# Up-projection of a two-part float32 feed-forward: high weights against the tokens' high and low parts in one product of 512 columns

## The reference, cut to what matters

```python
def squared_relu_mlp(x, w_up, w_down):
    return jnp.square(jax.nn.relu(x @ w_up)) @ w_down

def second_block(x, ...):
    h = x
    ...
    h = h + rms_norm_2(u, norm_mix_post[layer])
    u = squared_relu_mlp(rms_norm_2(h, norm_ffn_pre[layer]), w_up[layer], w_down[layer])
    h = h + rms_norm_2(u, norm_ffn_post[layer])
```

## Time and profile before

| | us |
|---|---|
| three runs | 970.64, 977.29, 977.51 |
| median | 977.29 |
| profiled execution: span from first to last instruction | 971.9 |
| profiled execution: its own time | not listed apart from the span |
| TensorE products busy | 934.8 (96%) |
| TensorE weight loads busy | 633.1 (65%) |
| VectorE busy | 443.5 (46%) |
| ScalarE busy | 351.2 (36%) |

### The profile page before, as it was taken

One profiled execution on the slowest core, in us unless ns is written; L12 is line 12 of the kernel. 1 busy time (PEld: TensorE's weight loads), 2 busy tenths in 40 slices (PEclk: granted clock), 3 DMA queues, 4 the chain that ended last, 5 costly groups with the idle time before them and its releaser, 6 DMA issues.

```text
span 971.9 us, 12898 instructions
## 1 busy us (share of the span) xinstructions
PE 934.8 (96%) x5259; PEld 633.1 (65%) x5259; DVE 443.5 (46%) x761; ACT 351.2 (36%) x568; POOL 25.9 (3%) x40
## 2 busy tenths in 40 slices
PE   7999999998999999999999999888999989999997
PEld 6979889885444443444434443333999889998886
DVE  5887665435232322223222322214776656655444
ACT  6745565532221121221212211115554454454332
POOL 1310000000000000000000000000000000000000
PEclk9999999999999999999999999999999999999999
DMA  9955553479999999999999999999944645555501
GB/s 317 359 191 170 172 173 130 173 272 409 401 429 426 426 428 430 424 430 427 428 428 425 428 427 430 426 428 374 355 154 153 196 129 175 174 182 205 176 1 44
DMA packets 72638, 289.81 MB, mean 298 GB/s; under 512 B 5121, under 2 KB 44673, under 8 KB 59650
## 3 DMA queue, kind: packets, MB, share of 16 engines
q1 hardware_dynamic: 72002, 288.79, 76.3%
q10 hardware_dynamic: 576, 0.17, 0.1%
HBM read 287.90 MB, written 1.05 MB: 297 GB/s over the span
## 4 chain that ended last, share of the span: by engine, by line
PE 83%; DMA 9%; DVE 3%; ACT 3%; issue 2%; POOL 0%; DVEq 0%; ACTq 0%
PE bank L1599 19%; PE bank L455 14%; PE bank L456 14%; PE bank L457 14%; PE bank L1621 10%; DMA ring<-in_w_gate_up_second 5%; DMA ring<-in_attn_w_qkv 4%; PE bank L1571 3%; PE bank L1637 3%; ACT w_high L520 1%; DVE w_low L552 1%; PE bank L755 1%; PE bank L793 1%; PE bank L510 1%; PE bank L1610 1%
## 5 line engine op out<-in xcount | busy, mean ns | idle before, releaser
L552 DVE TENSOR_TENSOR w_low<-ring,w_high 128x2048 fp32r<-128x2048 f32 x76 | 174.0, 2289 | 109.6 <-ACT w_high L520 109.5
L1599 PE MATMUL bank<-ring,arena 128*64 128x512 f32 x928 | 207.2, 595 | 7.3 <-DMA ring<-in_w_gate_up_second 6.0
L520 ACT ACTIVATE w_high<-ring 128x2048 fp32r<-128x2048 f32 x76 | 145.4, 1915 | 138.4 <-PE bank L457 136.2
L1599 PEld LDWEIGHTS bank<-ring,arena 128*64 128x64 f32 x928 | 64.8, 137 | 134.9 <-issue 116.9
L455 PE MATMUL bank<-xT_high,w_high 128*128 128x256 f32 x384 | 110.2, 287 | 1.1 <-DVE xT_low L563 1.1
L1736 DVE SCALAR_TENSOR_TENSOR y_low<-bank,arena,y_high 64x512 fp32r<-64x512 f32 x64 | 48.0, 750 | 138.0 <-ACT y_high L1671 137.5
L1621 PE MATMUL bank<-ring,arena 128*64 128x512 f32 x464 | 106.0, 598 | 4.4 <-issue 4.4
L456 PE MATMUL bank<-xT_low,w_high 128*128 128x256 f32 x384 | 109.2, 285 | 0.0
L457 PE MATMUL bank<-xT_high,w_low 128*128 128x256 f32 x384 | 109.2, 284 | 0.0
L1671 ACT ACTIVATE y_high<-bank,arena 64x512 fp32r<-64x512 f32 x64 | 43.7, 683 | 125.8 <-PE bank L1621 125.3
L1658 ACT ACTIVATE arena<-bank 128x256 f32<-128x256 f32 x32 | 12.3, 385 | 192.0 <-PE bank L1599 192.0
(11 more groups left out here) (296 smaller groups left out, 1496.2 us busy)
## 6 DMA issues: line engine op xcount, KB each, us to landing
ring<-in_w_down SPq DMA_DIRECT2D x28, 2048.0 KB, 28.8
ring<-in_w_gate_up_first SPq DMA_DIRECT2D x27, 2048.0 KB, 25.4
ring<-in_w_gate_up_second SPq DMA_DIRECT2D x27, 2048.0 KB, 26.8
ring<-in_w_down SPq DMA_DIRECT2D x18, 1024.0 KB, 5.0
ring<-in_w_up SPq DMA_DIRECT2D x16, 1024.0 KB, 5.3
ring<-in_attn_w_qkv SPq DMA_DIRECT2D x12, 1024.0 KB, 12.9
ring<-in_w_in SPq DMA_DIRECT2D x10, 1024.0 KB, 11.5
ring<-in_w_kv_mem SPq DMA_DIRECT2D x8, 1024.0 KB, 5.7
```

Of the source, the lines that this page charges most:

```text
L520: SC.activation(parts[buffer[0][u]][0][:, :], lanes[n % len(lanes)], ACT.Copy).then_inc(*high.inc(u))
L552: DVE.tensor_tensor(p[1][:, :], lanes[n % len(lanes)], p[0][:, :].bitcast(F32), ALU.subtract).then_inc(*split.inc(u))
L1599: last = PE.matmul(GU[t * SLOTS:(t + 1) * SLOTS, 0:NGU], xs[:, k, :], wgu[:, :, c, t * (DE // JT):(t + 1) * (DE // JT)], start=k == 0, sto ...
```

## The change

For each (n, k) of the up-projection the two products with the high weights (times `xT_high` and times `xT_low`) become one: the moving operand is an access pattern of two runs of 256 (`x_low_high[k]`), low part first, and the output takes a whole bank of 512 columns, low times high in columns 0 to 255, high times high in 256 to 511. The product with the low weights adds into columns 0 to 255 (the small half). So a unit has 16 products of 512 columns and 16 of 256, and two banks, f(i).0 and f(i).1, both opened before its first product. The moving operand's two runs need one tensor over both parts, so `xT_low` and `o_low` change places.

The two halves of a bank are summed as they leave: ScalarE copies the small halves to scratch (`small_sum`, new), VectorE adds the large halves onto them and gives back the banks, then makes the scaled maximum from scratch. Banks of the second block share their semaphores with those of the first (`Count(..., after)`), which frees semaphores for the new counts.

```diff
+f6.0@5 f6.1@6 f7.0@7 f7.1@0 f8.0@1 f8.1@2 f9.0@3 f9.1@4 f10.0@5 f10.1@6 f11.0@7 f11.1@0 f12.0@1 f12.1@2 f13.0@3 f13.1@0
+f14.0@4 f14.1@5 f15.0@6 f15.1@7
...
-    bank2 = Banks(nc, SECOND_BANKS, "second_")
-    xT2 = [chunks(rounded("xT_high", 2048, arena_at + 2 * TILE)), chunks(rounded("xT_low", 2048, slot_at(2)))]
+    bank2 = Banks(nc, SECOND_BANKS, bank1)
+    x_span2 = rounded("xT_low_high", (arena_at + 2 * TILE - slot_at(2) - TILE) // 4 + 2048, slot_at(2) + TILE)
+    xT2 = [chunks(x_span2[:, x_span2.shape[1] - 2048:]), chunks(x_span2[:, 0:2048])]
+    x_low_high = [bass.AP(tensor=x_span2, offset=xT2[1][:, k, :].offset,
+                          ap=[xT2[1].ap[0], [x_span2.shape[1] - 2048, 2], [1, S]]) for k in range(KC)]
...
+        def wide_features(u, ready=(), chunk_ready=()):
+
+            PE.wait_ge(*split2.at(u))
+            w_high, w_low = [t[:, :].rearrange("p (c n) -> p c n", c=KC) for t in parts2[buffer2[0][u]]]
+            into = [open_bank(bank2, f"{u}.{n}") for n in range(2)]
+            order = [(n, k) for n in range(2) for k in range(KC)]
+            if ready:
+                order.sort(key=lambda nk: nk[1] // HALF)
+            for n, k in order:
...
+                o = slice(n * P, (n + 1) * P)
+                PE.matmul(into[n][:, :].rearrange("p (l t) -> p l t", t=S), w_high[:, k, o], x_low_high[k], start=k == 0,
+                          stop=False, skip_group_check=True)
+                last = PE.matmul(into[n][:, 0:S], w_low[:, k, o], xT2[0][:, k, :], start=False, stop=k == KC - 1,
+                                 skip_group_check=True)
+            last.then_inc(*unit2.inc(u))
...
+        def small_sum(i):
+            SC.wait_ge(*unit2.at(f"f{i}"))
+            for n in range(2):
+                last = SC.activation(scratch(2 * (i % 2))[:, n * S:(n + 1) * S], banks[bank2.bank[f"f{i}.{n}"]][:, 0:S],
+                                     ACT.Copy)
+            last.then_inc(*small_sums.inc(i))
...
-            SC.wait_ge(*bank2.freed(f"f{i}"))
+            SC.wait_ge(*kept_rows.at(i))
...
+            small_sum(i)
             squared_high(i)
...
         def norm_kept(i):
 
-            if i >= 2:
-                DVE.wait_ge(*sq_high.at(i - 2))
             DVE.wait_ge(*unit2.at(f"f{i}"))
-            DVE.scalar_tensor_tensor(
-                out=scratch(2 * (i % 2)).rearrange("p (n t) -> p n t", t=S),
-                in0=banks[bank2.bank[f"f{i}"]][:, :].rearrange("p (n t) -> p n t", t=S), scalar=0.0,
-                in1=row["r2"].rearrange("p (n t) -> p n t", n=1).to_broadcast([P, 2, S]), op0=ALU.max,
-                op1=ALU.mult).then_inc(*bank2.inc(f"f{i}"))
+            kept = scratch(2 * (i % 2)).rearrange("p (n t) -> p n t", t=S)
+            DVE.wait_ge(*small_sums.at(i))
+            for n in range(2):
+                DVE.tensor_tensor(kept[:, n, :], banks[bank2.bank[f"f{i}.{n}"]][:, S:2 * S], kept[:, n, :],
+                                  ALU.add).then_inc(*bank2.inc(f"f{i}.{n}"))
+            for n in range(2):
+                DVE.wait_ge(*bank2.freed(f"f{i}.{n}"))
+            DVE.scalar_tensor_tensor(out=kept, in0=kept, scalar=0.0,
+                                     in1=row["r2"].rearrange("p (n t) -> p n t", n=1).to_broadcast([P, 2, S]), op0=ALU.max,
+                                     op1=ALU.mult).then_inc(*kept_rows.inc(i))
```

More of the change, by code:

```diff
@@ L27, with __init__ @@
 class Count:
[L30 to L35, removed]
+    def __init__(self, nc, name, order, after=None):
+        self.sem = after.sem if after else nc.alloc_semaphore(name)
+        self.made = after.total if after else 0
+        self.value = {key: self.made + n for n, key in enumerate(order, 1)}
+        self.total = self.made + len(self.value)
     def at(self, key):
@@ L61, with __init__ @@
 class Banks:
-    def __init__(self, nc, plan, prefix):
+    def __init__(self, nc, plan, after=None):
         turn, kept, self.bank = list(range(8)), {}, {}
@@ L82, in __init__ @@
                 kept[name] = b
-        self.free = [Count(nc, f"{prefix}bank{b}_free", uses[b]) for b in range(8)]
+        self.free = [Count(nc, f"bank{b}_free", uses[b], after.free[b] if after else None) for b in range(8)]
     def freed(self, name):
@@ L148 @@
 SECOND_BANKS = """
-+z0@0 +z1@1 +z2@2 +z3@3 -z0 -z1 -z2 -z3
-pT00@4 pT01@5 pT10@6 pT11@7 +v0.0 +v0.1 -v0.0 -v0.1 q0 r1 k0 q1 s0 s1 k1 q2 t0 t1 s2 s3 k2 a0 a1
+pT00@4 pT01@5 pT10@6 pT11@7 +v0.0@0 +v0.1@1 -v0.0 -v0.1 q0 r1 k0 q1 s0 s1 k1 q2 t0 t1 s2 s3 k2 a0 a1
 q3 t2 t3 s4 s5 k3 a2 a3 +v1.0@4 +v1.1@5 t4 t5 s6 s7 +o.0.0@0 +o.0.1@1 +o.1.0@2 +o.1.1@3 -v1.0 -v1.1
 a4@6 a5@7 t6@4 t7@5 a6@6 a7@7 -o.0.0 -o.0.1 -o.1.0 -o.1.1
-fT00@4 fT01@5 fT10@6 fT11@7 f0 f1 r2 f2 f3 f4 f5 f6 f7 f8 f9 f10 f11 f12 f13 f14@0 f15@7
+fT00@4 fT01@5 fT10@6 fT11@7 f0.0@0 f0.1@1 f1.0@2 f1.1@3 r2@4 f2.0@5 f2.1@6 f3.0@7 f3.1@0 f4.0@1 f4.1@2 f5.0@3 f5.1@4
+f6.0@5 f6.1@6 f7.0@7 f7.1@0 f8.0@1 f8.1@2 f9.0@3 f9.1@4 f10.0@5 f10.1@6 f11.0@7 f11.1@0 f12.0@1 f12.1@2 f13.0@3 f13.1@0
+f14.0@4 f14.1@5 f15.0@6 f15.1@7
 +y.0.0@0 +y.0.1@1 +y.1.0@2 +y.1.1@3
@@ L457, in three, with features @@
         return PE.matmul(o, ll, rh, start=False, stop=stop, skip_group_check=True)
-    def features(u, plan, split, unit, parts, buffer, x, ready=(), pairs=slice(0, 2 * KC), chunk_ready=None):
+    def features(u, plan, split, unit, parts, buffer, x, ready=(), pairs=slice(0, 2 * KC)):
         PE.wait_ge(*split.at(u))
@@ L2088, in build_program @@
     sq_low = Count(nc, "squared_low", range(NF))
+    small_sums = Count(nc, "small_sums", range(NF))
+    kept_rows = Count(nc, "kept_features", range(NF))
     added = Count(nc, "added", [f"{t}{h}{j}" for t in ("a", "y") for h in range(NH) for j in range(2)])
@@ L2189, in second_tensor @@
         for h in range(NH):
-            turn_sum("pT", h, XN, [bank2.freed(f"z{2 * h + j}") for j in range(2)], "pT")
+            turn_sum("pT", h, XN, [bank1.freed(f"acc{2 * h + j}") for j in range(2)], "pT")
         open_pair("v0")
@@ L2249, in second_tensor @@
             if i == 0:
-                f("f0", xT2, (("fT00",), ("fT01", "fT11")),
-                  [split2.at(f"eT10.{c}") for c in range(3)] + [bank2.freed("fT10")])
+                wide_features("f0", (("fT00",), ("fT01", "fT11")),
+                              [split2.at(f"eT10.{c}") for c in range(3)] + [bank2.freed("fT10")])
             else:
-                f(f"f{i}", xT2)
+                wide_features(f"f{i}")
             if i == 1:
@@ L2511, in second_vector @@
         DVE.wait_ge(*q.at("scattered", NE // 2))
[L2512 removed]
+        DVE.tensor_scalar(XN[:, 1, 0:512], banks[2][:, :], 1.0, None, ALU.mult).then_inc(*bank1.inc("acc2"))
         DVE.wait_ge(*z_gained.at("columns"))
```

26 lines of the change are left out of this document (14 added, 12 removed).

## The result

The changed kernel takes 983.84 us in the median of four runs (982.65 to 987.17), the kernel before 976.75 (970.64 to 977.51, the three runs told and one more beside). The recorded ratio is **1.0109, 95% interval 1.0087 to 1.013**: slower by about 1%. The two medians are 7.1 us apart, 0.7%, less than the ratio says; the four runs of the kernel before lie 6.9 us apart, so the size is known less well than the sign. The profiled span went from 971.9 to 983.3 us, 11.4 more; the profiled execution after took 984.53. All that follows accounts for the spans.

A forecast was written before the change was run, and what follows sets the result against it. The prediction took TensorE's column streaming to bound the up-projection, and after the change the late low weights. Stalls of 11.69 us less 3.35 saved, 8.3 more, added to the 977.3 median gave 985.6 us, range 975.5 to 990.

The forecast's parts named there:

- The chain: Up-projection: from a unit's end through ScalarE and VectorE to the product needing the low weights, 6.63 us against a 5.55 unit.
- The idle times: TensorE's stalls at f3, f5, f7, f9, f11, f13, f15 and y1, 11.69 us in all.
- The clock: Rival at f13: TensorE's clock falls in the 3.71 us wait, costing 1.6 us, 987.2 in all; chance 0.26.
- f13's hole: TensorE's wait before f13 for the bank that held f11's second half, 3.71 us.
- The saving: TensorE in the up-projection: 16 wide and 16 narrow products a unit instead of 48 narrow, 3.35 us saved.
- the chain doesn't bind: Rival in the up-projection: low weights don't delay TensorE; 977.7, or 973.9 without the bank wait too; chance 0.10.
- the clock falls at every stall: Rival: TensorE's clock drops at each stall, eight times 1.6 us, 998 in all; chance 0.05.
- a wide product costs 0.24: Rival: a 512-column product takes 0.24 us instead of 0.227, so nothing is saved, 987.7; chance 0.08.
- the loads bind: Rival: weight loads limit the up-projection, so fewer of them save 31 us, 946 in all; chance 0.01.
- the last two rivals: Clock falling often (998, chance 0.05) and loads binding (946, chance 0.01), the cases said to lie outside the range.

The follow-up runs named there:

- e2_banks: The changed kernel with another bank plan for f2 to f15, so f13 no longer needs f11's bank: 981.86 us, ratio 1.0096 to the kernel before.
- e5_fill: The changed kernel with 12 idle products on f13's first bank before TensorE waits for the second: 983.60 us, ratio 1.0102 to the kernel before.
- e4_sum_twice: The changed kernel with ScalarE's copies of the small halves made twice, order unchanged: 990.44 us, ratio 1.017 to the kernel before.
- e3_both: The changed kernel with ScalarE's copies ahead of the weights' high part and banks planned by fours: 970.02 us, ratio 0.9964 to the kernel before.
- e7_narrow: The kernel of `e3_both` with each wide product taken apart into two of 256 columns: 973.45 us, ratio 0.9992 to the kernel before.
- e8_low_first: The changed kernel with VectorE making the low part of f(i+3) ahead of the sum of f(i): 994.65 us, ratio 1.02 to the kernel before.
- e1_sum_first: The changed kernel with only ScalarE's copies moved ahead of the high part of f(i+3)'s weights: 970.65 us, ratio 0.9975 to the kernel before.

## Why the prediction was right, and where it was off

The forecast was 985.6 us in a range of 975.5 to 990; it is 983.84. The sign of the change and its cause were as written. That the time came so close is in part luck. The forecast added 8.3 us to a median of 977.29 from three runs 7 us apart, and the spans then grew by 11.4. In the other runs an execution takes 1.2 to 1.3 us longer than its span, so the profiled one before took an estimated 973.1; that and 11.4 give the 984.5 measured. A base 4 us too high and a change 3 us too small nearly cancelled. Step by step:

- **The chain.** Reckoned 6.63 us from the end of a unit to the product that waits for the low part. Measured for f11: ScalarE starts at 848.35 and f11's first product at 854.72, 6.37 later; the start of ScalarE is some 0.25 behind the end of the unit (866.02 + 0.12 to 866.39): 6.62. Its parts were off both ways: VectorE starts 0.1 behind the copies and 0.1 behind its own adds, where I had 0.03 each, and TensorE 0.05 behind VectorE, where I had 0.15.
- **The idle times.** Reckoned 11.69 us at f3, f5, f7, f9, f11, f13, f15 and y1; measured 11.5, at these eight and at no other place. f13's was 3.71 in both.
- **The clock.** I gave the case in which the clock holds through f13's hole 0.40 and the one in which it falls 0.26, and forecast the first. The second came: 1.65 us, reckoned 1.6. `e2_banks` and `e5_fill` show it from both sides, the hole gone and the hole filled, each with the clock at 1.00. This is the step that failed. The evidence is four traces with such a hole or its remedy, one execution each: holes of 3.7 us in the changed kernel and 4.1 in `e4_sum_twice` with half clock behind them, and the clock at 1.00 in the two kernels in which the hole is gone or filled.
- **The saving.** Reckoned 3.35 us. In the changed kernel 1.7 of it is there: idle time of 11.5 and the clock's 1.65 make 13.15, and the two stages are 11.4 longer (10.1 in the up-projection, where "about 7" was forecast, and 1.3 in the down-projection). What is missing lies between the stops. Two units take 11.21, 11.21, 11.41, 11.32 and 11.42 us from start to end (f3 to f12, from the starts above) where I had 11.10; f15 takes 5.76 for 5.55, and f0 to f2 18.59 for 18.33. That is 1.5. Some 0.7 of it is a price of stopping that the sum didn't have. Behind a wait the first wide product (its record is 0.50 long in the rows above) is followed by the next product after 0.34 us instead of 0.23, as at f3, which starts at 805.38:

```profile
805.72 0.27 PE L2145 MATMUL bank<-xT_low_high,w_low 128*128 128x256 f32 x1
```

That is 0.11 at each of f3, f5, f7, f9, f11 and f15. Another 0.14 is f0, which takes 7.16 us against 7.17 before and so saved 0.01 where I had 0.15. The rest stays open. `e3_both` has 5.55 from f3 on, and against `e7_narrow` its stretch from f3 to y1 is 2.75 us shorter. So the term is right for the product by itself and too large for a kernel that stops.
- **The rivals.** That the chain doesn't bind, that the clock falls at every stall (it stood at 1.00 around the seven short ones), that a wide product costs 0.24 and that the loads bind are all answered by the traces: no. The first of them had two times, and the lower, 973.9, lay outside the range, though the prediction says that only the last two rivals do. On the loads, the section "Identifying the Most-Contended Engine" of the Trainium skill's "Perfetto Trace Analysis" takes the busy share of weight loads as a measure of TensorE's headroom. Read as in the prediction it would give a third of the stage; this case doesn't agree, since the loads fell from 768 to 512 and `e3_both` gained 0.2 us a unit.

What the forecast lacked in sum: 8.3 reckoned, plus 1.65 for the clock, plus 1.65 of saving that did not come, gives 11.6 for the 11.4 measured between the spans.

## What to carry to other kernels

Before you add work to an engine because it is half idle, write down what it is idle for: if it stands between two halves of a chain that another engine waits for, the place of the new instruction in the queue decides first, and only in the wrong place does its length cost. Here the same instructions are 1.1% slower in one order and 0.3% faster in another, by the ratios. Put work on a result that is already there ahead of the wait for one that is still to come. A bank that is freed a step later is found again where the plan of banks is tightest.

## What I had not expected of the hardware

- One hole of 3.7 us with no product at all was followed by 3.4 us at 1.2 GHz, and one of 4.1 us in `e4_sum_twice` by 3.4 us too. In the 8.4 us hole of `e8_low_first` the granted clock is 0.50 from 873.4 us on, within the hole, until about 883.5. The seven waits of 1.0 to 1.3 us in the changed kernel stand at 1.00 throughout.
- The head of f0 shows that the clock isn't fixed by the program alone. With the same waits of 1.57 and 1.05 us ahead, f0 starts at 0.50 for some 3 us before and after the change, for some 6 in `e3_both` (788.2 to 794.2), and at 1.00 in `e1_sum_first` and `e5_fill`.
- The same program's runs differ by 0.7% on one chip and 0.8% on the other, and the longer ones mostly have the lower mean clock: in the runs of the kernel before beside the first experiments the span is 969.6 us where the mean granted clock is 0.997 and 975.8 where it is 0.990. Where the clock is low in these runs isn't shown, since they have no trace.
- A pair of products takes 0.347 us in `e3_both` throughout. In the changed kernel, with the 0.11 behind each stop taken off, it takes 0.347 in f3 to f6 and 0.350 to 0.353 in f7 to f12 (11.21 to 11.42 less 0.11, for 32), at a granted clock of 1.00 in both. What makes this difference stays open; no run was made for it.
